# Weight loads two blocks ahead on the sync queue, and the hidden layer's squares behind the next stage's bank copies

## The reference, cut to what matters

```python
xn = rms_norm(x, norm_mix_w)
proj = xn @ w_in                 # 1024 x 8208
# split into da_q, da_k, da_v, ml_q, ml_k, ml_v, ml_i, ml_f, ml_o, gate_pre
ya = rms_norm(diff_attention(da_q, da_k, da_v)) * 0.8 @ w_proj_a   # 8 heads
yb = (sigmoid(ml_o) * rms_norm(mlstm_chunkwise(...))) @ w_proj_b   # 8 heads
g  = sigmoid(gate_pre)           # 1024 x 2 x 1024
h  = x + (g[:, 0] * ya + g[:, 1] * yb) @ w_out
u  = relu(rms_norm(h, norm_ffn_w) @ w_ff1)                         # 1024 x 4096
h  = h + (u * u) @ w_ff2
return rms_norm(h, final_norm_w)
```

## Time and profile before

| what | value |
| --- | --- |
| median of the runs | 2068.0 us |
| the profiled execution's own time | 2073.0 us |
| its span | 2071.0 us |
| mean granted clock of TensorE | 0.977 |
| TensorE matmuls | 1943.2 us, 94%, 9378 instructions |
| TensorE weight loads (beside the matmuls) | 1619.5 us, 78% |
| VectorE | 1171.6 us, 57% |
| ScalarE | 963.8 us, 47% |
| GpSimd | 362.2 us, 17% |
| DMA | 300.17 MB, queue q1 at 49.4% of 16 engines |
| loads of `w_raw` from w_in, issue to landing | 9.2 us, median of 56 |

### The profile page before, as it was taken

The page is one execution under the profiler, slowest core; times in us unless marked ns, Lnnn a source line. Parts: engine busy times, 40 slices in busy tenths (PEclk is TensorE's granted clock), DMA queues, the critical chain, the costliest instruction groups (busy, mean ns, idle before and its releaser), DMA issues. The chain is left out here.

```text
span 2071.0 us, 26144 instructions
## 1 busy us (share of the span) xinstructions
PE 1943.2 (94%) x9378; PEld 1619.5 (78%) x9378; DVE 1171.6 (57%) x1537; ACT 963.8 (47%) x1633; POOL 362.2 (17%) x204
## 2 busy tenths in 40 slices
PE   5899989898999999998999999998989889999998
PEld 4778878686878887887788888877868778888886
DVE  5635655556566656651332112388667666788874
ACT  4446554554555555543433323225665655533331
POOL 0111111121211212112112444440000000021002
PEclk9999999899999999999999999999999999999999
DMA  6663545646262625355346444556476675754422
GB/s 185 142 183 79 138 87 98 110 77 146 51 176 52 175 47 161 62 159 83 69 71 189 154 137 150 188 181 234 169 259 206 222 251 181 245 197 157 165 81 82
DMA packets 210128, 300.17 MB, mean 145 GB/s; under 512 B 37096, under 2 KB 127848, under 8 KB 203136
## 3 DMA queue, kind: packets, MB, share of 16 engines
q1 hardware_dynamic: 197824, 290.37, 49.4%
q10 hardware_dynamic: 12224, 8.72, 1.3%
HBM read 207.75 MB, written 91.29 MB: 144 GB/s over the span
## 5 line engine op out<-in xcount | busy, mean ns | idle before, releaser
L708 PE MATMUL gp<-r1h,w_hi 128*128 128x512 f32 x1152 | 462.9, 402 | 29.7 <-ACT ev L1049 25.1
L709 PE MATMUL gp<-r1l,w_hi 128*128 128x512 f32 x1152 | 455.7, 396 | 0.0
L710 PE MATMUL gp<-r1h,w_lo 128*128 128x512 f32 x1152 | 455.5, 395 | 0.0
L1950 POOL TENSOR_TENSOR w_lo<-w_raw,w_hi 128x1024 fp32r<-128x1024 f32 x88 | 216.5, 2461 | 934.4 <-ACT w_hi L1044 934.4
L708 PEld LDWEIGHTS gp<-r1h,w_hi 128*128 128x128 f32 x1152 | 221.1, 192 | 77.9 <-ACT ev L1049 18.5
L710 PEld LDWEIGHTS gp<-r1h,w_lo 128*128 128x128 f32 x1152 | 220.3, 191 | 47.5
L709 PEld LDWEIGHTS gp<-r1l,w_hi 128*128 128x128 f32 x1152 | 221.0, 192 | 42.8
L964 PE MATMUL scores<-xh,qh 128*128 128x512 f32 x512 | 204.8, 400 | 25.6 <-DVE ql L1766 23.7
L966 PE MATMUL scores<-xl,qh 128*128 128x512 f32 x512 | 202.9, 396 | 0.0
L968 PE MATMUL scores<-xh,ql 128*128 128x512 f32 x512 | 202.4, 395 | 0.0
L1044 ACT ACTIVATE w_hi<-w_raw 128x1024 fp32r<-128x1024 f32 x88 | 93.1, 1058 | 153.3 <-DMA w_raw<-in_w_in 112.9
(11 more groups left out here) (328 smaller groups left out, 3715.2 us busy)
## 6 DMA issues: line engine op xcount, KB each, us to landing
xraw<-xo_d SPq DMA_DIRECT2D x54, 1024.0 KB, 5.3
proj_d<-ev SPq DMA_DIRECT2D x128, 256.0 KB, 2.5
rq<-in_w_ff SPq DMA_DIRECT2D x32, 1024.0 KB, 8.3
w_raw<-in_w_in SPq DMA_DIRECT2D x56, 512.0 KB, 9.2
xo_d<-res SPq DMA_DIRECT2D x78, 256.0 KB, 2.5
xo_d<-ring SPq DMA_DIRECT2D x60, 256.0 KB, 3.0
xtok<-in_x SPq DMA_DIRECT2D x16, 512.0 KB, 4.0
pr<-proj_d SPq DMA_DIRECT2D x16, 512.0 KB, 4.4
```

Of the source, the lines that this page charges most:

```text
L708: pe.matmul(gp[half][:], wh[slot][:, k, :], mh[:, k, t], start=(k == 0), stop=False)
L709: pe.matmul(gp[half][:], wh[slot][:, k, :], ml[:, k, t], start=False, stop=False)
L710: mm = pe.matmul(gp[half][:], wl[slot][:, k, :], mh[:, k, t], start=False, stop=(k == KT - 1))
L1950: pool.tensor_tensor(wl[slot][:], raw[slot][:], wh[slot][:].bitcast(F32), ALU.subtract).then_inc(w_split, 1)
```

## The change

It has two parts.

**Weight loads.** In a head round SP's iteration b now begins with `store(n-2)`, then loads weight block n+2 (in the last iterations of a round the first blocks of the next round, or gate blocks after the last), and only then come the reloads and stores of x, the gate rows and the attention's loads. Blocks 0, 1 and 2 are loaded during the first pass over x. The last head round is taken out of the hardware loop, so that it can load gate blocks 0 and 1 (`gate_load`). In the gate iterations the order is likewise store, load of block j+2 (the last two being the first blocks of w_proj_a), stage-ins, attention's loads. Buffers, sizes and the waits of `wload` stay as they are.

**Squares.** The squares of stage 1 move behind the copies of stage 2 in ScalarE's program, and the stores of what they make move on SP from stage 1 to stage 2.

```diff
             for j in range(TT + XB):
+                if j == TT:
+                    wload_head(0, 2)
                 x_load(j)
...
-            def head_round(h, att, first=False):
+            def head_round(h, att, first=False, last=False):
                 for b in range(HB):
-                    if not (first and b < 2):
-                        wload_head(h, b)
+                    if b >= 2 or not first:
+                        store(h * HB + b - 2)
+                    if b + 2 < HB:
+                        if not (first and b == 0):
+                            wload_head(h, b + 2)
+                    elif last:
+                        gate_load(b + 2 - HB)
+                    else:
+                        wload_head(h + 1, b + 2 - HB)
                     if isinstance(h, int):
...
                         sp.dma_start(inter_d, wrow[:]).then_inc(uw_st, 16)
-                    if b >= 2 or not first:
-                        store(h * HB + b - 2)
                     if att is not None:
...
+            def gate_load(j):
+                if j < 16:
+                    wload(N_GATE + j, j % 2, col_block(w_in2, OFF_G + j * P))
+                else:
+                    wload(N_GATE + j, j % 2, col_block(w_pa, (j - 16) * P))
...
-            with sp.Fori(2, NH) as h:
+            with sp.Fori(2, NH - 1) as h:
                 head_round(h, h - 1)
+            head_round(NH - 1, NH - 2, last=True)
             for j in range(16):
-                n = N_GATE + j
-                wload(n, n % 2, col_block(w_in2, OFF_G + j * P))
+                store(N_GATE + j - 2)
+                gate_load(j + 2)
                 if j == 13:
...
-                store(n - 2)
                 if j == 0:
                     att_loads(NH - 1)
...
+            for i in STAGE_AT[15]:
+                stage_in(i, oa_d[i])
             for k in range(2):
-                wload(N_PA + k, k, col_block(w_pa, k * P))
-                for i in STAGE_AT[15] if k == 0 else ():
-                    stage_in(i, oa_d[i])
                 store(N_PA - 2 + k)
...
             def hidden_stores(g, idx):
...
-                    if idx == 1:
+                    if idx == 2:
                         sp.wait_ge(u_done, done + u + 1)
...
-                    if idx == 1 and g < GROUPS:
-                        act.wait_ge(ev_b, 3 * UN * g + u + 1)
-                        relu_square(3 * UN * g + u, res[:, u, lo])
                     if idx == 2:
...
                         copied(s, u, res[:, u, hi])
+                for u in range(UN if idx == 2 and g < GROUPS else 0):
+                    act.wait_ge(ev_b, 3 * UN * g + u + 1)
+                    relu_square(3 * UN * g + u, res[:, u, lo])
```

More of the change, by code:

```diff
@@ L1378, in hidden @@
                         copied(s, u, res[:, u, hi])
+                for u in range(UN if idx == 2 and g < GROUPS else 0):
+                    act.wait_ge(ev_b, 3 * UN * g + u + 1)
+                    relu_square(3 * UN * g + u, res[:, u, lo])
+                for u in range(UN):
                     if idx == 3:
```

## The result

The changed kernel takes 2033.7 us in the median of 4 runs (2030.78 to 2035.84), the kernel before 2067.53 (2065.81 to 2070.8): ratio 0.983, 95% interval 0.981 to 0.985, so 34 us faster. The forecast was 2009, with a range of 1984 to 2030: the direction was right, the size too large by 25 us, and the result lies 3.7 us outside the range. The profiled execution took 2032.07 us (span 2030.3), 41 us less than that of before, against 59 forecast.

What follows compares the result with a forecast made beforehand. The prediction took TensorE, 94% busy, to bound the kernel. Stages 34, rounds 36 and gate round 10, less 21 at the start, gave 59 us off the profiled 2073.0: 2014, or 2009 against the median; range 1984 to 2030.

Steps and rivals of the forecast that it cites:

- Squares behind the copies: Stages, groups 0 to 3: TensorE's waits for late bank copies go, worth 26 us in groups 1 to 3, 8 in group 0.
- The margin of 1.2 us before stage 4: Stages: the first copy of stage 3 would end at 1529.6, wanted by TensorE at 1530.8, the thinnest margin there.
- rival (c): Stages: the 1.2 us margin or stage 6's operand load is missed in each group, costing 16 us: 2025, chance 0.12.
- The start: First round: stores of transposed x queue behind weight loads, delaying ScalarE's copies and head 0's attention: 21 us lost.
- Rival (a): Start: it is cheap, as weight loads land fast enough and the stores of x interleave: 1981, chance 0.15.
- the estimate of 1.2: Weight loads: by the skill's 435 GB/s, a 512 KB block takes 1.2 us to move and the start loses nothing.
- The two projection loads and `stage_in` at the end only change places under a busy TensorE: nothing: End of the gate round: reordering these loads costs and gains nothing.
- Gate round: Gate round: a 7.45 us wait for `evac` and 2.6 us lost at low clock go: 10 us, bounds 7 and 12.
- Rounds: Six head rounds: earlier weight loads end ScalarE's waits, 37.5 us less 1.5 for late rows: 36, bounds 15 and 40.
- The undisturbed round of 104.8 us: Head rounds: the shortest round, 107.77 us, less its 1.38 and 1.61 us waits; six such total 628.8 us.
- Rival (b): Head rounds: they give half, as rows or values behind early loads become ScalarE's last wait: 2029, chance 0.16.
- From profile to median: Whole kernel: the profiled execution lay 5 us over the median of 2068.0, so 2014 became 2009.

Runs made afterwards that it cites:

- e3_xfirst: The changed kernel with the first pass's load of block n+2 put behind the reloads and stores of x and the two gate rows: 2009.34 us.
- e4_stagein: The changed kernel with the next product's operand loads again in front of the weight load in the last three gate iterations: 2021.53 us.
- e8_rows: The changed kernel, weight loads behind first-pass stores of x and last three gate iterations' operand loads, u and inter loads before block 4's: 1992.67 us.
- e10_actq: e8_rows with the weight loads of all head rounds and of the gate round up to block 62 issued on ScalarE's queue: 1997.85 us.
- e11_source: e8_rows with the weight blocks of head rounds and gate round read from w_ff1, not w_in, so the output is another: 1976.25 us.
- e1_squares: The kernel before with only the squares moved behind the copies, weight loads left where they were: 2039.39 us against 2071.59.
- e12_offset: e11_source with every block read 16 columns (64 B) further on, so the output is computed from other columns: 1976.41 us.

## Why the forecast was too large, step by step

- **Squares behind the copies: right**, in mechanism and size: 35.0 us in the profile, 32 timed, forecast 34. The comparison with group 4, which has no squares there, carried it. The margin of 1.2 us before stage 4 held; rival (c) did not come.
- **The start: right.** 23.2 us lost, forecast 21: the store lands behind the load, ScalarE's copy waits for it, and head 0's attention comes late. TensorE stood 4.9, 8.4 and 3.3 us behind the copies and 9.7 us before L797, and e3_xfirst gave it back by moving the loads of these iterations behind the stores. Rival (a) falls. The shortest load of 4.0 us that stood for it was one from w_out, and the row's median of 8.6 is mixed in the same way: from w_in the shortest took 5.7 us and the median 9.2, in before. The Trainium skill, DMA: Bandwidth & Descriptors, section Specifications, whose line rate would have made the start free, does not agree with the trace of the kernel after: its fastest weight load of 512 KB took 3.7 us against the estimate of 1.2, its fastest from w_in 5.6, and the median from w_in 9.2.
- **"The two projection loads and `stage_in` at the end only change places under a busy TensorE: nothing": wrong, and the largest miss.** This is the step that failed: a term put at nothing. It cost 8.4 us, 9.5 by e4_stagein. I had priced exactly this (a transfer behind a weight load) in the start, and did not ask it of `stage_in`, though the cover that I named, a busy TensorE, hides nothing from ScalarE. There ScalarE waited 11.48 us for the operand, the high part of the operand stands in front of `evac`, and TensorE then waited 3.19 and 2.57 us.
- **Gate round: 7.4 instead of 10**, the edge of its bounds of 7 to 12. The wait of 7.45 us became 2.14, not nothing: `evac` then waits 6.95 us for a store of `ev` that was issued behind a weight load, and took 14.2 us.
- **Rounds: 29.9 instead of 36**, inside the bounds of 15 to 40. The queue I walked through held keys, values, `ckq`, `osig` and the rows; I gave the rows 1.5 us. They cost 3 in round 3 and 1 in round 4 (e8_rows). The stores of `ev` were missing from that list, though each stands behind a load of the iteration before; with the loads issued at other times the two rounds that they lengthen fell by 1.9 and 1.4 us (e10_actq against e8_rows). The undisturbed round of 104.8 us was right: with loads that land in 3.9 us (e11_source) all six take 104.3 to 104.4, together 40 us less than before. Rival (b) named this kind of cause, but at three times its size, and only for rows and values.
- **From profile to median:** I took 5 us off, because the profiled execution of before lay that much over its median. That of after lies 1.6 us under its own, so 6.6 of the 25 us come from there. The fastest and the slowest of 17 runs of before, timed beside e1_squares, lie 15 us apart (2063.38 to 2078.48), so the distance of one execution to the median should at least have widened the range.

By the windows: 8.4 + 6.1 + 2.6 + 2.2 - 1.0 = 18.3 us, and 6.6 for the median, make the 25.

## What to carry to other kernels

When a large load is moved forward in the program that issues it, list everything behind it, stores included, and for each the engine that waits for its landing and what stands behind that engine's wait; "TensorE is busy" is no cover for another engine's queue. Put behind the load only what has more free time than the load takes to land, and count the load's own wait, at which the issuing engine stands. Another queue by itself is no way out: in e10_actq the stores landed behind the loads all the same. When a load is slow, compare it with one of the same size and pieces from another tensor before working around it: here another source tensor was worth 16 us on top of the best order, though it computes something else.

## What the runs showed of the hardware that was not expected

- Loads of 512 KB in 512 B pieces landed in 9.3 us (median of 56, e8_rows) from w_in, with rows of 32832 B, and in 3.9 (e11_source) from w_ff1, with rows of 16384 B, in the same places of the same order; starting 64 B further on changed nothing (4.0, e12_offset).
- A store issued while such a load has 3 us or more to go lands behind it, also when the load was issued from the other engine's queue: 35 of 35 stores of `ev` in e8_rows, with both in SP's queue, and 23 of 24 in e10_actq, with the loads in ScalarE's. Alone such a store takes 2.0 us.
- The stores of x landed in 3.7 us in the median before the change and in 11.1 after it, where each was issued while a weight load was on its way.
